# Eight ring slots for the experts' weights, and smaller steps at the entry and at the stage borders

## What is computed

```python
def moe_ffn(x, router, w_gu, w_down):          # 8 experts, 3584 wide, two chosen per token
    logits = (xt @ router).astype(jnp.float32)
    top_v, top_i = lax.top_k(logits, TOP_K)
    w = jax.nn.softmax(top_v, axis=-1)
    ...
    for e in range(N_EXPERTS):
        y = y + combine[:, e:e + 1] * swiglu(xt, w_gu[e], w_down[e])
```

## Time and profile before

| | us |
|---|---|
| median of 3 runs | 2191.95 (2181.12 to 2200.92) |
| profiled execution | 2186.8 |
| its span, first to last instruction | 2184.1 |
| PE busy | 2014.8 (92%) |
| DVE busy | 1204.8 (55%) |
| ACT busy | 971.2 (44%) |
| mean granted PE clock | 0.966 |
| DMA moved | 524.40 MB, 240 GB/s over the span |

### The profile page before, as it was taken

One profiled execution on the slowest core, in us unless ns is written; L12 is line 12 of the kernel. 1 busy time (PEld: TensorE's weight loads), 2 busy tenths in 40 slices (PEclk: granted clock), 3 DMA queues, 4 the chain that ended last, 5 costly groups with the idle time before them and its releaser, 6 DMA issues.

```text
span 2184.1 us, 27826 instructions
## 1 busy us (share of the span) xinstructions
PE 2014.8 (92%) x10836; PEld 1485.2 (68%) x10836; DVE 1204.8 (55%) x1356; ACT 971.2 (44%) x1140; POOL 21.0 (1%) x33
## 2 busy tenths in 40 slices
PE   8889999998999999999988889998999899989997
PEld 7667998776899788877766566655555555555553
DVE  5965555686655654575667344444544445444454
ACT  5454444545444344445544244443443334343443
POOL 0000000000000000000000000000000000000000
PEclk9989999999999999999798899999999999999999
DMA  7414554431655355543103589997999899988995
GB/s 274 145 49 144 189 176 155 172 135 48 223 194 192 125 209 183 186 154 101 40 1 135 228 342 395 373 409 298 380 372 406 316 354 386 391 356 346 395 403 223
DMA packets 74665, 524.40 MB, mean 240 GB/s; under 512 B 8768, under 2 KB 9216, under 8 KB 12192
## 3 DMA queue, kind: packets, MB, share of 16 engines
q1 hardware_dynamic: 71712, 511.64, 60.8%
q0 software_dynamic: 2816, 10.93, 1.5%
HBM read 521.49 MB, written 1.05 MB: 239 GB/s over the span
## 4 chain that ended last, share of the span: by engine, by line
PE 76%; DVE 13%; ACT 7%; issue 3%; DMA 1%; DVEq 0%; SPq 0%; ACTq 0%
PE psum L548 54%; PE psum L2802 9%; PE psum L2853 4%; DVE LO L2748 3%; ACT HI L2741 2%; DVE AR L1710 1%; PE psum L924 1%; PE psum L987 1%; PE psum L2923 1%; ACT HI L531 1%; PE psum L2102 1%; DMA ring<-in_experts 1%; PE psum L729 1%; PE psum L748 1%; DVE AR L941 1%
## 5 line engine op out<-in xcount | busy, mean ns | idle before, releaser
L548 PE MATMUL psum<-HI,XT 128*128 128x512 f32 (+1 forms) x2080 | 538.0, 402 | 37.7 <-ACT HI L2741 21.1
L548 PEld LDWEIGHTS psum<-HI,XT 128*128 128x128 f32 x2080 | 394.4, 195 | 164.6 <-issue 49.5
L539 DVE TENSOR_TENSOR LO<-ring,HI 128x2048 fp32r<-128x2048 f32 (+1 forms) x157 | 346.8, 2214 | 284.8 <-ACT HI L531 284.8
L531 ACT ACTIVATE HI<-ring 128x2048 fp32r<-128x2048 f32 (+1 forms) x157 | 289.7, 1849 | 230.1 <-PE psum L548 229.6
L2748 DVE TENSOR_TENSOR LO<-ring,HI 128x2048 fp32r<-128x2048 f32 x112 | 255.4, 2290 | 217.3 <-ACT HI L2741 215.5
L548 PE MATMUL psum<-LO,XT 128*128 128x512 f32 (+1 forms) x1040 | 283.8, 396 | 12.2 <-DVE LO L2748 12.1
L2741 ACT ACTIVATE HI<-ring 128x2048 fp32r<-128x2048 f32 x112 | 213.1, 1909 | 168.1 <-DMA ring<-in_experts 148.6
L548 PE MATMUL psum<-HI,HTH 128*128 128x512 f32 x568 | 228.2, 402 | 32.7 <-ACT HI L2741 32.7
L548 PEld LDWEIGHTS psum<-LO,XT 128*128 128x128 f32 x1040 | 199.6, 195 | 57.1 <-DVE LO L2748 15.8
L548 PE MATMUL psum<-HI,HTL 128*128 128x512 f32 x568 | 222.1, 391 | 0.0
L548 PEld LDWEIGHTS psum<-HI,HTH 128*128 128x128 f32 x568 | 106.6, 188 | 80.5 <-ACT HI L2741 40.4
(11 more groups left out here) (317 smaller groups left out, 1864.8 us busy)
## 6 DMA issues: line engine op xcount, KB each, us to landing
ring<-in_experts SPq DMA_DIRECT2D x224, 1024.0 KB, 8.0
ring<-in_dense SPq DMA_DIRECT2D x149, 1024.0 KB, 4.8
AR<-in_experts SPq DMA_DIRECT2D x112, 1024.0 KB, 8.7
bcs<-in_ln_g POOLq DMA_DIRECT2D x4, 512.0 KB, 4.5
bcs<-in_ln_b POOLq DMA_DIRECT2D x4, 512.0 KB, 5.1
bcs<-in_norm_g POOLq DMA_DIRECT2D x3, 512.0 KB, 3.8
cons<-in_cons POOLq DMA_DIRECT2D x1, 1317.0 KB, 8.0
X<-in_x SPq DMA_DIRECT2D x2, 512.0 KB, 3.9
```

The lines of the kernel that those rows point to most:

```text
L531: e.activation(HI[:, h:h + m], slot(u), ACT.Copy).then_inc(*high.up(u))
L539: e.tensor_tensor(LO[:, h:h + m], slot(u), HI[:, h:h + m].bitcast(F32), ALU.subtract).then_inc(*(freed if u in early else low).up(u))
L548: ins = e.matmul(out_ap, lhsT=a, rhs=b, start=start and n == 0, stop=stop and n == len(pairs) - 1)
```

## The change

- `DEEP = 8`: slot 6 lies over constants that are no longer used then (`SPENT`, the constants from `ones` on; the table of constants is put in another order so that those still used lie ahead), slot 7 in the area of the norm vectors (`bcs`). Slot 7 is used up to expert unit 303, then seven slots go round; GpSimd loads the last norm's vectors after that unit. SP waits for the router's unit before an expert unit goes into a slot that has had none.
- In memory an expert's up and gate units alternate by halves of the input, as the stages take them, so the first chunk needs no order of its own. `plan` has one set of rows instead of two, `table_vector` gets its two instructions per stage from `table_turn_vector`, which runs between the `first_lo` casts; `TABLE` moves to `TMP2`. The side that isn't taken follows (`paired_cols`).
- Chunk 0 of every stage: great up and gate of half 0, in stage 0 then the fetch of the few tokens and the first few columns, great up and gate of half 1, then the second expert's few columns for both halves. `few_cols` loses its special case for the first chunk.
- The fetch of the few tokens leaves the entry of PE and ACT and stands in chunk 0.
- Putting back in halves: quarters 0 and 1 in chunk 0, quarters 2 and 3 in chunk 1, and the small matmuls quarter by quarter. Weights one chunk later for stages 1 to 3, lists and slots in chunk 2, the fetch in chunks 3 to 6.
- One HI and one LO of each chunk move forward: on ACT ahead of the few columns' eviction, on DVE right behind the product with the gate.

```diff
@@ -20,7 +20,7 @@
 KB = D // P
 UNIT = 2048
 NSLOT = 4
-DEEP = 6
+DEEP = 8
 NHL = 3
 AHEAD = 2
 NEG = -1.0e30
@@ -364,14 +369,13 @@
     return np.concatenate([r.reshape(-1) for r in rows_of[:dense]]), experts, shapes, at
 
 
-def stage_units(s):
+def stage_units():
 
 
     units = []
     for c in range(9):
-        if (s, c) == (0, 0):
-            units += [(0, p, c, i) for p in ("up", "gate") for i in range(2)]
-            units += [(1, p, c, i) for i in range(2) for p in ("up", "gate")]
+        if c == 0:
+            units += [(w, p, c, i) for w in range(2) for i in range(2) for p in ("up", "gate")]
         elif c < 7:
             units += [(w, p, c, i) for i in range(2) for w in range(2) for p in ("up", "gate")]
         if c >= 2:
@@ -496,7 +501,8 @@
 
         slots, count, latest = [], [0] * DEEP, [-1] * DEEP
         for u in range(len(units)):
-            i = u % NSLOT if u < dense else (u - dense) % DEEP
+            n = u - dense
+            i = u % NSLOT if n < 0 else n % DEEP if n < 304 else (n - 304) % (DEEP - 1)
             count[i] += 16
             slots.append((i, latest[i], count[i]))
             latest[i] = u
@@ -504,7 +510,9 @@
         def slot(u):
 
             i, m = slots[u][0], units[u][0] * units[u][1]
-            return ring[:, i * UNIT:i * UNIT + m] if i < NSLOT else A(11776 + (i - NSLOT) * UNIT, m)
+            if i < NSLOT:
+                return ring[:, i * UNIT:i * UNIT + m]
+            return (A(11776, m), A(13824, m), SPENT, bcs[:, 0:UNIT])[i - NSLOT]
 
         def landed(u):
             i, _, n = slots[u]
@@ -2876,20 +2896,17 @@
                     few_turn_tensor(e, s, w, c)
 
         def stage_cols(e, s, c):
-            if (s, c) == (0, 0):
+            for i in range(2):
+                for part in ("up", "gate"):
+                    great_cols(e, s, part, c, i)
+                if (s, c, i) == (0, 0, 0):
+                    fetch_few_tensor(e)
+                if FEW[s][0]:
+                    few_cols(e, s, 0, c, i)
+                if c:
+                    few_cols(e, s, 1, c, i)
+            if c == 0:
                 for i in range(2):
-                    great_cols(e, s, "up", c, i)
-                for i in range(2):
-                    great_cols(e, s, "gate", c, i)
-                for w in range(2):
-                    for i in range(2):
-                        few_cols(e, s, w, c, i)
-            else:
-                for i in range(2):
-                    for part in ("up", "gate"):
-                        great_cols(e, s, part, c, i)
-                    if FEW[s][0]:
-                        few_cols(e, s, 0, c, i)
                     few_cols(e, s, 1, c, i)
 
         def tiles_of(s):
@@ -2907,7 +2924,7 @@
                 ins.then_inc(*filled.up("lists", s, b))
 
         def fetch_few_tensor(e):
-            bank = banks.take(e, "fetch", 0, 0)
+            bank = banks.hold(e, BA[0], "fetch", 0, 0)
             e.wait_ge(*v_done.of("slots", "stage", 0))
             for k in range(KB):
                 for t in range(2):
@@ -2924,13 +2941,13 @@
                                    rhs=ONE[:, t, :], start=t == 0, stop=t == 1)
             ins.then_inc(*filled.up("fetch", s, kp))
 
-        def put_back_tensor(e, s):
-
-            quarter = [banks.take(e, "scatter", s, q) for q in range(4)]
+        def put_back_tensor(e, s, h):
+
+            quarter = {q: banks.take(e, "scatter", s, q) for q in (2 * h, 2 * h + 1)}
             few = [w for w in range(2) if FEW[s][w]]
             for b in range(0, len(tiles_of(s)), 2):
                 e.wait_ge(*a_bank.of("lists", s, b))
-            for q in range(4):
+            for q in quarter:
                 e.wait_ge(*a_bank.of("acc", s, q // 2))
                 for t in range(2):
                     e.matmul(quarter[q][:, t * S:t * S + S], lhsT=LISTS[:, 0, tile(t)],
@@ -2938,16 +2955,16 @@
             for w in few:
                 n = FEW[s][w]
                 e.wait_ge(*a_bank.of("acc few", s, w))
-                for r in range(n // 32):
+                for q in quarter:
+                    g, r = divmod(q, n // 32)
                     for t in range(2):
-                        for g in range(P // n):
-                            q, last = g * (n // 32) + r, w == few[-1] and t == 1
-                            ins = e.matmul(quarter[q][:, t * S:t * S + S],
-                                           lhsT=LISTS[g * n:(g + 1) * n, 1 + w, tile(t)],
-                                           rhs=YF[g * n:(g + 1) * n, w, r * S:r * S + S], start=False,
-                                           stop=last)
-                            if last:
-                                ins.then_inc(*filled.up("scatter", s, q))
+                        last = w == few[-1] and t == 1
+                        ins = e.matmul(quarter[q][:, t * S:t * S + S],
+                                       lhsT=LISTS[g * n:(g + 1) * n, 1 + w, tile(t)],
+                                       rhs=YF[g * n:(g + 1) * n, w, r * S:r * S + S], start=False,
+                                       stop=last)
+                    if last:
+                        ins.then_inc(*filled.up("scatter", s, q))
 
         def put_last_tensor(e, s):
             e.wait_ge(*a_bank.of("lists", s, 0))
@@ -2967,12 +2984,12 @@
             for s in range(STAGES):
                 for c in range(7):
                     stage_cols(e, s, c)
-                    if c == 0 and s:
-                        put_back_tensor(e, s - 1)
-                    if c == (1 if s else 0):
+                    if c < 2 and s:
+                        put_back_tensor(e, s - 1, c)
+                    if c == (2 if s else 0):
                         lists_tensor(e, s)
-                    if 2 <= c < 6 and s + 1 < STAGES:
-                        stage_fetch_tensor(e, s + 1, c - 2)
+                    if c >= 3 and s + 1 < STAGES:
+                        stage_fetch_tensor(e, s + 1, c - 3)
                     if c >= 1:
                         stage_turn(e, s, c - 1)
                     if c >= 2:
@@ -3134,22 +3150,30 @@
                 for c in range(7):
                     if c == 0 and s:
                         few_out_scalar(e, s - 1, 1)
-                    part_hi(e, 2 if c == 0 else 3)
+                    if (s, c) == (0, 0):
+                        part_hi(e)
+                        e.wait_ge(*filled.of("fetch", 0, 0))
+                        e.wait_ge(*a_order.last)
+                        e.activation(XF[:, 0], banks.get("fetch", 0, 0).rearrange("p (k s) -> p k s", k=KB),
+                                     ACT.Copy).then_inc(*a_bank.up("fetch", 0, 0))
+                        part_hi(e)
+                    else:
+                        part_hi(e, 3 if c else 2)
                     great_up_scalar(e, s, c)
+                    part_hi(e)
                     for w in range(2):
                         if FEW[s][w]:
                             few_cols_scalar(e, s, w, c)
-                    if c == (1 if s else 0):
+                    if c == (2 if s else 0):
                         lists_scalar(e, s)
                     if (s, c) == (0, 1):
                         residue(e, 1)
-                    if 2 <= c < 6 and s + 1 < STAGES:
-                        stage_fetched_scalar(e, s + 1, c - 2)
-                    if c >= 2:
-                        part_hi(e)
+                    if c >= 3 and s + 1 < STAGES:
+                        stage_fetched_scalar(e, s + 1, c - 3)
                     if c >= 1:
                         stage_turn_scalar(e, s, c - 1)
-                    part_hi(e, 2 if c >= 2 else 1)
+                    if c >= 2:
+                        part_hi(e, 2)
                 stage_turn_scalar(e, s, 6)
                 part_hi(e, 3)
                 great_out_scalar(e, s)
@@ -3174,15 +3198,10 @@
             e.activation(sm(1, "root"), EPS[:, 0:1], ACT.Silu).then_inc(*a_done.up())
             for kp in range(4):
                 first_hi(e, kp)
-            split_hi(e)
-            e.wait_ge(*filled.of("fetch", 0, 0))
-            e.wait_ge(*a_order.last)
-            e.activation(XF[:, 0], banks.get("fetch", 0, 0).rearrange("p (k s) -> p k s", k=KB),
-                         ACT.Copy).then_inc(*a_bank.up("fetch", 0, 0))
-            split_hi(e, AHEAD - 1)
-            e.wait_ge(*v_done.of("many"))
             for s in (a_bank, a_done):
                 s.mark("end", -1)
+            split_hi(e, AHEAD)
+            e.wait_ge(*v_done.of("many"))
             all_experts(e, expert_scalar, last_scalar, stages_scalar)
             begin(e, ("end", "sides"), (a_bank, a_done))
             first_root(e)
@@ -3452,19 +3474,19 @@
                 for c in range(7):
                     part_lo(e, 2 if c == 0 else 3)
                     great_gate_vector(e, s, c)
-                    if c == 0:
-                        if s:
-                            put_back_vector(e, s - 1)
```

(38 more changed lines are left out.)

110 lines of the change are left out of this document (61 added, 49 removed).

## The result

| | before | after |
|---|---|---|
| median | 2189.19 us (2181.12 to 2200.92, 4 runs) | 2093.52 us (2091.71 to 2096.46, 4 runs) |
| profiled execution, span | 2186.8, 2184.1 | 2096.46, 2094.4 |
| order DMA to end of span | 999.9 | 906.4 |
| PE busy | 2014.8 (92%) | 1996.8 (95%) |

The ratio is 0.956, with a 95% interval of 0.9514 to 0.9607. The forecast was 2119 us with a range of 2095 to 2152: the sign and the main mechanism hold, the gain is larger than the range allowed for.

A forecast was written before the change was run, and what follows sets the result against it. The prediction took PE (TensorE) as the bound, stalled by work order on ACT and DVE. Entry, stages and tail summed to 927.0 us against 1000.1, -73 us, giving 2119 us against the median 2191.95; range 2095 to 2152.

The forecast's parts named there:

- main mechanism: Chunks 2 to 6: HI and LO made before the few experts' evictions end PE's stalls, 20 x 1.7 to 1.9 us.
- the landing rival: Chunk stalls: slots come free late, the early HI waits for its DMA, 2152 us; chance 0.14.
- the memory limit: Expert stages: DMA capped near 367 GB/s, so 2181 us and no measurable change; chance 0.05.
- the slower case: ACT: the early HI waits for late landings and holds up evictions, turn and silu, 2221 us; chance 0.03.
- The sum, from busy PE time in the earlier trace: Expert stretch: old PE busy times plus corrections per stage, 927.0 against 1000.1, -73 us.
- clock and scatter terms: Borders: most of 2.5 us of slow clock goes; reordered small putting-back matmuls cost +4.5 once, +1.7 at the other two.
- Putting back in two halves: Stage borders: bank wait (0.8), LO wait (3.72) and most of the slow clock (2.5 us) go.
- I take +4.5 for the border of stages 0 and 1: Putting back there: small matmuls following each other in one row group lose overlap, +4.5 us, near the serial end.
- In steady chunks this gives nothing by itself ... six would just do: Eight slots in steady chunks: landings already 5 us or more ahead of use, gain 0.
- The residue's 3.3 us: Chunk 1 at the entry: ACT scales the residue before the turn and second HI, a returning wait of 3.3 us.
- the 18.7 us of the entry: Entry with first two chunks: earlier PE start, fewer waits and faster clock start chunk 2 at 1243, not 1261.7: -18.7.
- The low end, 2095: Range's lower bound: putting back overlaps (-8), entry at full clock (-6), small waits absent (-8).

The follow-up runs named there:

- The late HI: The changed kernel with HI and LO of chunks 2 to 6 put back behind the evictions: 2142.15 us, ratio 0.9796.
- three moves: Changed kernel with putting-back quarters alternating row groups, residue's second half two chunks later, stage-end HI after half the accumulators' eviction: 2083.33 us.

## Why the prediction was right and wrong

Right: PE was the bound and memory wasn't. The order of HI and LO on ACT and DVE is the greatest term, in both directions (-59.6 when it alone is changed, +48.9 when chunks 2 to 6 alone are changed back). Landings kept up with eight slots, and neither the landing rival nor the memory limit nor the slower case came about. Of the signs set out, the small matmuls (4.20 and 3.98 us a border) came as said and the plain chunks a little shorter (30.6 and 29.2 to 29.7 us for 31.2 and 29.8); stages 1 and 2 came out under 224 to 227. PE's first expert product came at 1197.64, past the 1197 that was to speak against the prediction, but in a profile whose dense half had ended 3.85 us later than before's. The Trainium skill, "DMA: Bandwidth & Descriptors", Specifications, gives about 358 GB/s as HBM's limit per core (a stack's 716, halved for two cores); the trace disagrees, with 388 to 414 over the stages of after and 421 over 210 us in the kernel with fewer LO products. By the page's figure stage 1 alone would have taken an estimated 246 us (84 units of 1.048576 MB); it took 220.9.

Wrong by 20.5 us in the stretch (927.0 forecast, 906.4 measured), in these steps:

- "The sum, from busy PE time in the earlier trace rows". PE's busy time was taken as fixed work. It fell by more than the clock and scatter terms explain: stage 2 from 222.74 to 218.75, where the sum had 221.9. A stall costs more than its wait, 0.6 us in each of 20 chunks, some 12 of the 20.5 us. The late HI shows it by itself: 2.45 us per chunk for 1.87 of recorded waits.
- "Putting back in two halves": 0.8, 3.72 and 2.5 us a border were credited to the halves. Beside an early LO they are worth nothing (+0.3 without them). The same edit on DVE that the prediction had counted for chunks 2 to 6 alone carried the borders too, 20.4 us over all chunks 0 and 1. The gain was there, put down to the wrong part.
- "I take +4.5 for the border of stages 0 and 1": it was +2.2 (4.20 us against 2.01). Neighbours of 32 rows in one group cost 131 ns, not the 231 of a full-height matmul. The other two, +1.7 forecast, were +2.0. The Trainium skill, "TensorEngine Tiling (Array Packing)", Key Properties, has tiles work in parallel; the 64-row pairs agree (249 to 141 ns), while 32 rows in two groups gained next to nothing (131 to 125) and in four 63.
- "In steady chunks this gives nothing by itself ... six would just do": right in stages 1 and 2, wrong in stage 0. Of the 29.4 us that six slots cost, 10 are in chunk 0 and some 14 in the chunks behind it. The count took slots as freed in order of use at an even pace; in stage 0 the great ones come free only behind the few columns.
- The residue's 3.3 us were added twice, in the 18.7 us of the entry (10.8 - 4.2 + 5.8 + 7.8 - 3.3 - 2 + 4 is 18.9) and again in the rest of stage 0. The trace has one wait of 2.21 us, at 1249.01, in the rest of stage 0. As much was missed at the entry (55.7 against 59.0), where the other errors nearly cancel. PE's first product came 9.6 us behind the order DMA, 1.8 later than forecast: the last cast of XT and the first HI ended 6.5 and 6.65 us behind it, as forecast, but 3.0 us and not 1.0 passed from there to PE's start (why is open). Against that the small waits came to 1.0 us instead of 2, and the fetch to 3.68 instead of 4.2. The 4 us from the clock came as forecast (0.95 granted in chunks 0 and 1 instead of 0.85). The fetch's move is worth 10.2 us, where the prediction had 10.8 - 4.2 = 6.6.
- The low end, 2095, had terms for the scatter, the clock and small waits. None let a stall cost more than its row, and those 12 us alone are more than the 1.5 us by which the median lies under it.

What is left open: of the 4.5 us that order of units, fetch, borders and entry give together at six slots, the shares weren't tried, and the 0.4 us between two profiles are all that is known of the noise of a stretch.

## What to carry to other kernels

Ahead of a wait that an engine will sit out anyway, put the work that the next engine needs; price the stall by the time of one loop pass with and without it, since here the wait row held only 1.87 of the 2.45 us. Moving such work forward needs buffers deep enough for it, or it becomes the head of a line: the same edit wants six slots or eight depending on how late a stage frees them. When two edits could each remove a wait, undo them one at a time before crediting either.

## What had not been expected of the hardware

- DMA held 420 to 421 GB/s over 420 us in a row, as soon as TensorE had less to do, and no slice of any page shows more than 422.
- Small matmuls of 32 rows in one row group took 131 ns each, of 64 rows 249, of 128 rows 249. Two groups in turn brought 64 rows to 125 (before) and 141 (three moves), 32 rows only to 125; four groups brought 32 rows to 63.
- The dense half, the same in all kernels, ended anywhere between 1181.5 and 1195.2 us in thirteen profiles, a spread larger than most parts of this change: span differences of single profiles don't show them.
